# Moving conv taps beside the gated unit's products, and interleaving the query products of cross attention

## The reference

```python
def cross_attention(h, mem_n, wq, wk, wv, wo):       # 4 heads of 256, 256 memory rows
    q = (h @ wq).reshape(bsz, seq, X_HEADS, X_HEAD_DIM)
    ...
    s = jnp.einsum('bqhd,bkhd->bhqk', q, k).astype(jnp.float32) * (X_HEAD_DIM ** -0.5)
    p = jax.nn.softmax(s, axis=-1)
    o = jnp.einsum('bhqk,bkhd->bqhd', p.astype(v.dtype), v).reshape(bsz, seq, D_MODEL)
    return o @ wo

def second_block(...):                               # for each of 2 layers
        mod = c_act @ w_ada[l] + b_ada[l]            # shift, scale, gate: 1024 each
        ...
        y_conv = conformer_conv(u_val, u_gate, conv_w[l], ...) * jax.nn.silu(g_conv)
        y_attn = dsa_attention(c_q, c_kv, k_idx, w_idx, ...) * jax.nn.silu(g_attn)
        y = jnp.concatenate([y_conv, y_attn], axis=-1) @ w_out[l]
        x = x + gate[:, None, :] * rmsnorm(y, g_post[l])
```

## Time and profile before

| | us |
|---|---|
| median of 3 runs (1802.95, 1803.03, 1807.79) | 1803.03 |
| the profiled execution | 1807.16 |
| its span, first to last instruction | 1805.8 |
| cross attention (from its query products to w_xo) | 439.71 to 534.77 |
| experts | 611 to 1110 |
| attention of the two layers | 1294 to 1405 and 1625 to 1737 |

### The profile page before, as it was taken

How to read it: one execution, slowest core, us unless ns; L and a number is a source line. 1 busy time by engine, 2 the same in 40 slices (tenths; PEclk the granted TensorE clock), 3 DMA queues, 4 the chain that set the end, 5 groups by cost and what they waited for, 6 DMA issues and landing times.

```text
span 1805.8 us, 15346 instructions
## 1 busy us (share of the span) xinstructions
PE 1629.6 (90%) x5808; PEld 795.6 (44%) x5808; DVE 738.5 (41%) x1525; ACT 483.4 (27%) x984; POOL 366.5 (20%) x348
## 2 busy tenths in 40 slices
PE   6699999999989799998788887999978999998898
PEld 3244446644454433333333333544455454445553
DVE  2916534345162411111010011469774143996622
ACT  2013243101031101000000002466365134645631
POOL 3610000100000111111110110148143012842500
PEclk9899999999999899889898889989999999999999
DMA  8321031456262699999999998401202120020101
GB/s 324 140 94 47 1 116 60 173 187 225 79 262 101 250 417 405 405 401 410 404 404 399 409 416 353 163 1 70 70 1 88 65 93 0 24 94 24 47 1 47
DMA packets 72977, 328.08 MB, mean 182 GB/s; under 512 B 10522, under 2 KB 13746, under 8 KB 60480
## 3 DMA queue, kind: packets, MB, share of 16 engines
q1 hardware_dynamic: 64976, 310.23, 44.2%
q0 software_dynamic: 6144, 10.52, 1.8%
q10 hardware_dynamic: 1776, 6.27, 0.9%
HBM read 320.60 MB, written 14.78 MB: 186 GB/s over the span
## 4 chain that ended last, share of the span: by engine, by line
PE 66%; DMA 20%; DVE 10%; ACT 2%; issue 1%; POOL 1%; DVEq 0%; ACTq 0%; POOLq 0%; SPq 0%
PE bank L187 62%; DMA arena<-in_w 15%; DMA arena<-h_rows,arena 3%; DVE arena L1264 2%; DVE arena L2551 1%; PE bank L2149 1%; DVE arena L2535 1%; PE bank L581 1%; POOL arena L1349 1%; DVE arena L2605 1%; DVE arena L2592 1%; DMA arena<-in_w_ada 0%; DMA arena<-in_params 0%; PE bank L666 0%; PE bank L906 0%
## 5 line engine op out<-in xcount | busy, mean ns | idle before, releaser
L187 PE MATMUL bank<-arena 128*128 128x512 f32 (+11 forms) x4944 | 1525.5, 551 | 100.4 <-DMA arena<-in_w 49.8
L187 PEld LDWEIGHTS bank<-arena 128*128 128x128 f32 (+5 forms) x4944 | 692.8, 178 | 865.6 <-issue 788.0
L2767 POOL TENSOR_TENSOR arena<-arena 128x512 f32<-128x512 f32 x180 | 205.2, 1140 | 223.7 <-ACT arena L2376 206.0
L1851 POOL TENSOR_TENSOR arena<-arena 128x1 f32<-128x1 f32 (+2 forms) x44 | 32.8, 746 | 598.3 <-DVE arena L1254 372.9
L1797 DVE TENSOR_TENSOR arena<-arena,bank 64x512 f32<-64x512 f32 x32 | 22.1, 691 | 314.0 <-ACT arena L1220 314.0
L2376 ACT ACTIVATE arena<-arena 128x512 f32<-128x512 f32 x180 | 126.2, 717 | 21.5 <-POOL arena L2767 21.3
L990 ACT COPY arena<-bank 128x512 f32<-128x512 f32 (+3 forms) x115 | 61.2, 538 | 248.6 <-PE bank L187 147.2
L1220 ACT ACTIVATE arena<-bank 64x512 f32<-64x512 f32 x32 | 18.9, 592 | 369.3 <-PE bank L187 369.3
L1872 POOL DMA_INDIRECT y_rows<-arena x32 | 32.1, 1004 | 413.4 <-PE bank L906 247.6
L1264 DVE SCALAR_TENSOR_TENSOR arena<-arena 128x512 f32<-128x512 f32 x84 | 78.4, 934 | 3.0
L1790 DVE TENSOR_TENSOR arena<-bank,arena 128x512 f32<-128x512 f32 x32 | 22.1, 692 | 112.0 <-PE bank L906 111.9
(11 more groups left out here) (264 smaller groups left out, 897.7 us busy)
## 6 DMA issues: line engine op xcount, KB each, us to landing
arena<-in_w SPq DMA_DIRECT2D x96, 2048.0 KB, 40.2
arena<-in_w_in SPq DMA_DIRECT2D x15, 2048.0 KB, 8.0
arena<-in_w_ada SPq DMA_DIRECT2D x12, 2048.0 KB, 9.2
arena<-in_w_out SPq DMA_DIRECT2D x6, 2048.0 KB, 7.7
arena<-in_w_xk SPq DMA_DIRECT2D x2, 2048.0 KB, 9.6
arena<-in_w_xv SPq DMA_DIRECT2D x2, 2048.0 KB, 10.6
arena<-in_w_xq SPq DMA_DIRECT2D x2, 2048.0 KB, 10.0
arena<-in_w_xo SPq DMA_DIRECT2D x2, 2048.0 KB, 9.1
```

The lines of the kernel that those rows point to most:

```text
L187: i = pe.e.matmul(o, l, r, start=first and j == 0, stop=last and j == len(pairs) - 1)
L2767: pool.e.tensor_tensor(yc, yc, k.prod[l][n % 4], ALU.add).then_inc(*k.pool.step("sum", l, f, j))
```

## The change

In cross attention only query products 0 to 3 stand ahead of the pipeline; products 4 to 7 follow one by one in its ticks 0 to 3, on ScalarE too. The scores of step s wait for query copy 2h + 1 rather than for all. Gate sum (0,1) is made in tick 6 and taken by VectorE in tick 7. The adaptive sum (1,0) moves behind VectorE's pipeline, gate sum (1,0) and adaptive sum (1,1) into the router after its first turn. POOL computes the root of router tile 0 ahead of the rows of (1,1).

In both layers the 17 taps inside the attention stand in four sets, of 5, 5, 4 and 3, at the ends of ticks 1, 5, 10 and 24.

```diff
@@ pe_cross
-    for n in range(2):
-        pe.wait_ge(*R.landed(("w_xq", n)))
-        for f in range(4):
-            pe_by_feature(k, pe, ("qx", 4 * n + f), A, R.at(("w_xq", n), 8, 512), f, k.HT)
-        pe_gate(k, pe, 0, n)
-    pe.wait_ge(*A.done("qx", 7))
+    pe.wait_ge(*R.landed(("w_xq", 0)))
+    for f in range(4):
+        pe_by_feature(k, pe, ("qx", f), A, R.at(("w_xq", 0), 8, 512), f, k.HT)
+    pe_gate(k, pe, 0, 0)
+    pe.wait_ge(*R.landed(("w_xq", 1)))
     for tick in range(7 + 6):
...
             if phase == 0:
                 b = B.take(pe, A, "xs", s)
+                pe.wait_ge(*A.done("qx", 2 * h + 1))
...
-    pe_gate(k, pe, 1, 0)
+        if tick < 4:
+            pe_by_feature(k, pe, ("qx", 4 + tick), A, R.at(("w_xq", 1), 8, 512), tick, k.HT)
+        elif tick == 6:
+            pe_gate(k, pe, 0, 1)
@@ pe_router
     pe_out(k, pe, "w_xo", k.OT, [(0, 0), (0, 1), (1, 0)])
     pe_router_turn(k, pe, 0)
+    pe_gate(k, pe, 1, 0, ROUTER_BANKS)
     pe_out(k, pe, "w_xo", k.OT, [(1, 1), (2, 0)])
@@ act_cross
+def act_qx(k, act, f):
+    act.wait_ge(*k.pe.done("qx", f))
+    act.e.activation(k.QX[:, f, :], k.banks.at("qx", f), ACT.Copy, scale=1.0 / 16).then_inc(*k.act.step("qx", f))
...
-    for f in range(8):
-        act.wait_ge(*P.done("qx", f))
-        act.e.activation(k.QX[:, f, :], B.at("qx", f), ACT.Copy, scale=1.0 / 16).then_inc(*A.step("qx", f))
+    for f in range(4):
+        act_qx(k, act, f)
...
+        if tick < 4:
+            act_qx(k, act, 4 + tick)
@@ dve_cross
     dve_ada(k, dve, 0, 2, 1, k.gacc)
-    dve_gate(k, dve, 0, 1)
-    dve_ada(k, dve, 1, 2, 0, k.gacc)
     for tick in range(7 + 6):
...
-    dve_gate(k, dve, 1, 0)
-    dve_ada(k, dve, 1, 2, 1, k.gacc)
+        if tick == 7:
+            dve_gate(k, dve, 0, 1)
+    dve_ada(k, dve, 1, 2, 0, k.gacc)
@@ dve_router, after the adds of each row tile
         if t < 2:
             dve_router_turn(k, dve, t)
+        if t == 0:
+            dve_gate(k, dve, 1, 0)
+            dve_ada(k, dve, 1, 2, 1, k.gacc)
@@ pool_first
     for l, n in GATES[1:]:
+        if (l, n) == (1, 1):
+            pool_root(k, pool, k.f_ss[:, 0:1], "f", 0)
         pool.wait_ge(*V.done("gg", *GATES[2 * l + n - 1]))
         pool_gate_rows(k, pool, l, n)
-    for t in range(4):
+    for t in range(1, 4):
         pool_root(k, pool, k.f_ss[:, t:t + 1], "f", t)
@@ constants of the layers
-PROD_AT, TAP_AT, TAPS = 8, 13, 14
+PROD_AT, TAPS = 8, 14
+TAPS_AT = {1: 5, 5: 5, 10: 4, 24: 3}
@@ dve_attend, at the end of each tick
-        if TAP_AT <= tick < TAP_AT + 31 - tap:
-            dve_taps(k, dve, l, tap + tick - TAP_AT, tap + tick - TAP_AT + 1)
+        if tick in TAPS_AT:
+            dve_taps(k, dve, l, tap, tap + TAPS_AT[tick])
+            tap += TAPS_AT[tick]
```

## The result

The changed kernel took 1792.92 us (median of five runs, 1785.89 to 1793.72) beside 1807.79 us of the kernel before on the same chip (1802.95 to 1815.02): ratio 0.9907, 95% interval 0.9886 to 0.9927. It is faster, by 15 to 17 us; the time lies above the range on record (1778.0 to 1789.5). The profiled execution took 1793.72 us, span 1792.4.

What follows compares the result with a forecast made beforehand. Bounds: TensorE in cross attention, weight transfers in the experts, TensorE and VectorE waiting for each other in the layers' attention. Cross attention 4.35 plus 15.6 us for both layers gives 19.95; 1803.03 less that is 1783.1 us, range 1778 to 1789.5.

Steps and rivals of the forecast that it cites:

- The wait of 3.68 us: Cross attention: TensorE idles after the query products until the first normalised tile, since VectorE is still in adaptive sum (1,0).
- the clock fall: Layer attention, 1337 to 1341: granted clock 0.68, expected full once TensorE's wait before it goes; 1.3 of the 7.8 us.
- the transposition wait of 1.02 us: Cross attention: TensorE's idle at the fifth transposition, forecast to remain at about 1.0 us behind VectorE's reduction of scores 7.
- the gate sum that comes back: Gate sum (1,0) returns as 0.87 us of TensorE among the w_xo products, leaving 4.35 of 5.2 us by the second turn.
- the turn by turn account: Cross attention: first four scores between query products 4 to 7, followed to w_xo's start at 529.55 instead of 534.77, 5.2 us.
- The taps until the last gated product: Each layer's attention: with taps in four sets, the row with the last gated product starts at 1343.2, 6.1 us won.
- The spill of the second set: Each layer: the second set of taps, 3.9 us, exceeds VectorE's 3.81 us wait by 0.1 us, counted as a loss.
- Rival (a): Layer attention: the clock falls all the same, as TensorE still waits; 1.3 us a layer less, 1785.7 us; chance 0.12.
- Rival (b): Layer attention: VectorE and POOL block each other in full, third set 0.7 us late a layer, 1784.5 us; chance 0.05.
- Behind it: Each layer behind the last gated product: 1.8 us won from 2.4 us of taps, TensorE's 2.1 us a pair taking over.
- rival (c): Layer attention: multiplies now meet POOL, 0.3 us more in ten pairs, 3 us a layer, 1789.1 us; chance 0.09.
- the base: Whole kernel: the 19.95 us won is subtracted from the median of 1803.03 us; 1787.9 if runs lie like the upper one.

Runs made afterwards that it cites:

- the version with its products under the gated product: Kernel after with the six ScalarE tap products of ticks 26 to 31 moved to ticks 1 and 24, later ones one a tick: 1787.06 us, ratio 0.9878 to before.
- Narrow sums: Kernel after with POOL's sums of ScalarE's tap products for the last channel group cut from 512 to 64 columns: layers of 74.10 and 74.08 us.

## Why the prediction was right or wrong

**Direction and mechanism: right.** Faster had 0.94. The wait of 3.68 us went, the taps left the chain, the clock fall went, and the halves are near the sizes on record: 4.16 against 4.35, 6.98 against 7.8.

**Cross attention: right in sum, with one reason too many.** 5.05 against 5.2 to w_xo, since the transposition wait of 1.02 us and a bare copy (0.68) stayed as worked out; 0.89 against 0.87 for the gate sum that comes back. The router weights arrived as forecast (first step 543.71, forecast about 542) and cost nothing. But the turn by turn account put query products between the scores to explain what moving the sums does without them.

**The taps until the last gated product: 6.7 us where 6.0 (6.1 less 0.1) stood.** The forecast times of the five transpositions, from 1329.23, were 1331.45, 1335.3, 1337.4, 1341.0 and 1342.8; they came, from 1329.54, at 1331.84, 1335.40, 1337.29, 1340.91 and 1342.58. Counted from their starts, which are 0.31 us apart, following pair by pair was good to 0.5 us over five pairs. The spill of the second set, counted at 0.1, is nothing. Rival (a), the clock, fell: the wait of 2.15 us became 0.58, not 1.4, and the clock is 1.00 there though waits of 0.58 and 1.02 us are left. The Trainium skill, TensorE: Matmul & The Clock Gate, has the rule on short idles, by which this rival was the likelier one, in its section A second HAM failure mode: psum-queue depth-cycling; in this stretch it didn't decide. Rival (b) fell too: the third set took 4.35 us and hid whole.

**Behind it: 0.26 where 1.8 stood. This term was mis-sized.** I took TensorE's 2.1 us a pair as what takes over from the taps, and a multiply beside POOL as 0.7. It is 0.99 to 1.35, because it waits for the end of a sum. That was rival (c), priced at 0.3 in ten pairs; in truth the meetings are few and dear, up to 0.9 each, and cost only where the multiply is on the path. Narrow sums show what the meetings with the last channel group's sums cost a layer, 3.0 us, and the version with its products under the gated product shows that 1.75 of it can be had back.

**The time: the base failed.** The step was "I subtract from the median". That median of three, 1803.03, lay low: the same three with two more on that chip have 1807.79, and 45 runs of the same kernel beside the experiments have a median of 1807.81 (1799.91 to 1817.57), and four of them are under 1803.1. The 9.8 us of the miss are 4.8 of base, 1.1 of the effect (19.95 against 18.9, the difference of the medians of all runs; by the traces' stretches 1.8), and 4.0 by which the five runs of after lay over the median of 15 (1788.93), rounded each. The base was a step that could be done better. The 4.0 are luck in which five runs came, as far as the runs show: the kernel before has the same median on that chip as on the others. As a ratio the forecast was 0.9889, and the whole change measured 0.9907, 0.9893 and 0.9889, each time with 0.9889 inside the interval. The trace had given the hint: the profiled execution took 1807.16, 4.1 above the median, and the text itself gave 1787.9 for runs of that kind and then treated it as the lesser case.

Where runs of one kernel part is seen from the three traces of the kernel after (spans 1792.4, 1787.6 and 1781.4). The first query product starts at 440.81, 438.67 and 432.66; then it is 126.19 us to the second turn in all three; from there to the last copy of the experts 541.71, 540.52 and 541.33; to the first transposition of the layers 201.61, 200.51 and 199.68; a layer 77.1 each time. 8.15 of the 11.0 us lie ahead of 440, where nothing was changed. Two places there, each in the longest execution (span 1792.4) and then in the shortest (1781.4). Timeline of TensorE:

```profile
86.91 52.74 PE L187 MATMUL bank<-arena 128*1 128x256 f32 x148 [4.34 <-DVE arena L1274]
```

```profile
84.18 51.12 PE L187 MATMUL bank<-arena 128*1 128x256 f32 x148 [1.15 <-DVE arena L1274]
```

Windows:

```profile
200.00:250.00 50.00, 48.21 (x146) 22.43 (x146) 23.53 (x66) 12.11 (x37) 0.00 (x0) 0.93 0.17 60
```

```profile
200.00:250.00 50.00, 48.14 (x160) 23.44 (x159) 23.43 (x60) 12.52 (x35) 0.00 (x0) 1.00 0.19 67
```

A wait for VectorE that is 3.2 us longer and a clock of 0.93 instead of 1.00 in one window are such places. What sets them from run to run was not tried and is open.

## What to carry to other kernels

Work of an engine that is off the path is free where another engine's long product lies over it, and costs most of its length two or three ticks away (2.6 to 3.8 us for sets of 3.7 to 3.9 here). Read the idle time ahead of the operation behind the gap, bundle the work to fit, and check whose work beside it makes it longer in that gap. Before work is moved later, look for who waits for its end. When filler work leaves a busy stretch, ask which operation will now meet the neighbour that the filler used to meet. Subtract a forecast from a median of many runs, or state it as a ratio: three runs that span 5 us don't carry an absolute time to 2.

## What the runs showed of the hardware

A 128x384 multiply on VectorE takes 0.41 us alone and up to 1.35 beside a 128x512 sum on POOL, and it ends 0.1 to 0.2 us behind that sum; five taps in a row take 3.90 us alone and 6.74 under a row of sums. And three executions of one kernel differ by 11 us in span, while the stretch of 126.19 us and the layers of 77.1 us repeat to 0.03 us: stage lengths of single traces told apart what five rounds of whole runs could not.
